# GpSimd's additions of squares behind the input and the mixing stages, and a wait in front of them

## The chip, the cores and the metric

The kernel runs on one core of one Trainium2 chip. The metric is the device time of one execution in microseconds, as the median of several runs. Names of the engines: TensorE (PE in the profile, PEld for its weight loads), VectorE (DVE), ScalarE (ACT), GpSimd (POOL), SyncE (SP, which issues the loads of weights here).

## The reference

Two small transformer blocks of two layers each, one after the other, on 256 tokens of width 1024 in float32. Cut to what matters here, a layer is

```python
def _rms(x, gain):
    y = x * rsqrt(mean(x * x, axis=-1) + EPS)
    return y * gain

x = x + 0.5 * swiglu(_rms(x, g0), w_in, w_out)      # feed-forward, hidden width 2816
x = x + mixing(_rms(x, g1))                         # a mixing stage
x = x + 0.5 * swiglu(_rms(x, g2), w_in, w_out)      # feed-forward
```

The four mixing stages are a gated linear recurrence (HGRN), a dilated attention, a stick-breaking attention and a sliding-window attention with sinks. Every norm needs the sum of the squares of the 1024 columns of x, for each token.

## The kernel before, in words

**Layout.** x lies transposed in SBUF, 8 chunks of 128 columns by 256 tokens, and is worked on in four pairs of chunks (NPAIR = 4). Float32 products are made of float32r parts: every operand is split into a high part and a low part (value less high part), and a product is high times high, high times low and low times high.

**Weights.** SyncE loads a stage's weights slot by slot, each slot in two halves, into `raw`. ScalarE copies a half into its high part (`split_high`, line 1304, tile `whi`), VectorE subtracts it to get the low part (`split_low`, line 1724, tile `wlo`, an operation on `raw` and `whi`). TensorE waits for the low part of the half that it is to use. The split of a slot is made two slots ahead of its use.

**Norm.** The scale of a norm is applied behind the product. So the input of a stage is only x times the gain: ScalarE makes its high part (`high_x`, line 1311, tile `xg`), VectorE its low part (`low_x`, line 1742, tile `xg`; operands x, the gain and the high part), chunk by chunk, and each low part raises the semaphore `xg_ready`. TensorE waits in the first slot of a stage for chunk after chunk. Beside it ScalarE squares each pair of chunks (line 1316): pair 0 into `acc`, pairs 1 to 3 into `sq`, `sq_two` and `newton`. GpSimd adds the three onto `acc` (`add_squares`, line 2227). TensorE sums `acc` over the partitions with a product with ones (`sum_squares`, lines 851 and 852), which waits for all additions. VectorE and ScalarE then make the reciprocal root `r` (lines 1748, 1324, 1326, 1752 to 1756).

**Behind a mixing stage** (and behind the input) comes a feed-forward. The four pairs of the output product come out shortly after one another at the end of the last output slot. VectorE adds pair m to x (line 1731; behind the input it is the copy of line 1729), then makes the two low parts of pair m-1, and behind pair 3 those of pairs 2 and 3. After them come, in VectorE's order, both weight halves of the second up slot (line 1724), the first half of the third, the sum of the first slot's gate (line 1797), which frees the first slot's bank, the second half of the third slot, the norm, the scaled gate (line 1802), a step of the sigmoid (line 1806), the first half of the fourth slot, and the sum of the second slot (line 1809), which frees the second slot's bank. The fourth slot uses that bank again. TensorE has `sum_squares` in the middle of the second up slot, between its two halves. An up slot is 8 chunks by 2 pairs of products (lines 839 and 840), 16 pairs in all.

**Behind a feed-forward** the pairs come out one by one, some 15 us apart, and GpSimd adds each as it comes (line 2227, called from `ffn`).

**GpSimd's order.** It adds the squares of the input first, and then goes through the layers; the adds of a mixing stage are the last of its work there, and the next on it is the gate work of the feed-forward behind (lines 2235, 2238, 2240), which waits for `r`. It issues no DMA.

Of the kernel before, what the change touches and what calls it, by code (L numbers as in the profile page):

```python
# [28 lines left out]
KC = D // P  # L29
# [4 lines left out]
NPAIR = KC // 2  # L34
# [98 lines left out]
def build_program(nc, io, upto=None):  # L133
# [6 lines left out]
    def sem(name):  # L140
        return ctx.enter_context(nc.semaphore(name))
# [56 lines left out]
    updates = [(n, us) for n, us in updates if n == "input" or n in stages]  # L198
    updates[-1] = (updates[-1][0], [])
    update_of = {name: e for e, (name, _) in enumerate(updates)}  # L200
    LAST = len(updates) - 1
    g_before, k_before = [], []
    for e in range(LAST + 1):
        g_before.append(KC * sum(u[0] == "g" for _, us in updates[:e] for u in us))
        k_before.append(KC * sum(u[0] == "k" for _, us in updates[:e] for u in us))
# [126 lines left out]
    xg_ready = sem("xg_ready")  # L332
# [51 lines left out]
    def pair(ap):  # L384
        return ap.rearrange("p (c t) -> p c t", c=2)

    def r_of(e):

        return r[:, e % 2:e % 2 + 1, :].broadcast_to([P, 2, T])

    def hidden(i, part):

        return hT[:, bass.ds(2 * i, 2), part, :]
# [1825 lines left out]
    def _(pool):  # L2219
# [3 lines left out]
        def add_squares(e, m):  # L2223

            pool.wait_ge(acc_done, NPAIR * e + m)
            pool.wait_ge(sq_done, (NPAIR - 1) * e + m)
            nc.gpsimd.tensor_tensor(acc[:, :], acc[:, :], squares_of[m][:, :], ALU.add).then_inc(acc_done, 1)  # L2227

        def ffn(f):
            st, e = stages[f"up{f}"], reads[f"up{f}"]  # L2230
            pool.wait_ge(r_ready, e + 1)
            with pool.Fori(0, FPAIRS) as i:
                p = FPAIRS * f + i
                pool.wait_ge(gate_made, p + 1)
                nc.gpsimd.tensor_tensor(pair(gate_r[:, :]), pair(gate[:, :]), r_of(e), ALU.mult).then_inc(gr_done, 1)  # L2235
                pool.wait_ge(gr_done, p + 2)
                pool.wait_ge(sig_ready, p + 1)
                nc.gpsimd.tensor_tensor(gate_s[:, :], gate_r[:, :], gate_s[:, :], ALU.mult).then_inc(gs_done, 1)  # L2238
                pool.wait_ge(hhi_done, p + 1)
                nc.gpsimd.tensor_tensor(hidden(i, 1), pair(h[:, :]), hidden(i, 0).bitcast(F32), ALU.subtract).then_inc(hT_ready, 1)  # L2240
            for m in range(1, NPAIR - 1 if update_of[f"down{f}"] == LAST else NPAIR):
                add_squares(update_of[f"down{f}"], m)

        def out_stage(name):
            for m in range(1, NPAIR):
                add_squares(update_of[name], m)

        def hgrn():
            nc.gpsimd.memset(hg_P[:, :, :], 0.0).then_inc(hg_zero, 1)
# [3 lines left out]
            for t in range(HG_TICKS):  # L2253
# [25 lines left out]
                for u in hg_units(t, 0):  # L2279
                    pool.wait_ge(hg_on, 2 * u + 2)  # L2280
                    pool.wait_ge(hg_gs, u + 1)
                    out = flat(hg_out[:, 2 * u:2 * u + 2, :])
                    nc.gpsimd.tensor_tensor(out, out, hg_g[:, :], ALU.mult).then_inc(hg_og, 1)
            out_stage("hgrn_out")


        def dil():
            st = stages["dil"]
            for point in range(2 * DL_TICKS):
                for hd in dl_due(point, DL_SCALE):  # L2290
                    pool.wait_ge(dl_rd, hd + 1)
                    own = dl_S[:, hd % 2, GROUPS * T:]
                    nc.gpsimd.tensor_tensor(own, own, dl_rcp[:, hd % 2, 0:1].broadcast_to([P, GROUPS * P]), ALU.mult).then_inc(dl_sc0, 1)
            out_stage("dil_out")


        def stick():
            out_stage("stick_out")
# [20 lines left out]
                    nc.gpsimd.tensor_tensor(own, own, sw_rcp[:, (u - 1) % 2, 0, :].unsqueeze(2).broadcast_to([P, 4, P]), ALU.mult).then_inc(sw_sc0, 1)  # L2319
            out_stage("swa_out")  # L2320

        for m in range(1, NPAIR):
            add_squares(0, m)
        for layer in layers:
            if layer.startswith("ffn"):
                ffn(int(layer[3:]))
            if layer == "hgrn":
                hgrn()
            if layer == "dil":
                dil()  # L2330
            if layer == "stick":
                stick()
            if layer == "swa_kv":
                swa_kv()
            if layer == "swa":
                swa()
# [34 lines left out]
```

## Time and profile before

| | us |
|---|---|
| median of 3 runs | 2165.11 |
| lowest, highest | 2163.71, 2165.37 |
| span of the profiled execution | 2161.0 |
| TensorE busy | 2126.5 (98%) |
| VectorE busy | 1607.5 (74%) |
| ScalarE busy | 1307.3 (60%) |
| GpSimd busy | 586.1 (27%) |

The profiled execution has no other time of its own than its span, from the first instruction to the last; the median of the runs is 4.1 us above it. How to read it: TensorE is almost never idle, so what matters is its few idle stretches. The row of the chain that ended last gives 90% of the span to TensorE, 5% to VectorE, 3% to ScalarE and 1% to GpSimd. A row of a timeline has the start, the duration (both in us), the engine, the line, the operation, the tiles written and read, the count of merged instructions, and in brackets the idle time before it with its releaser.

### The profile page before, as it was taken

To read this page: it belongs to the slowest core of one execution; us is meant where nothing else is said; L and a number is where in the kernel's file an instruction comes from. 1 tells how busy PE (TensorE), PEld (TensorE's weight loads), DVE (VectorE), ACT (ScalarE), POOL (GpSimd) and SP (SyncE) were. 2 spreads that over 40 slices of the span, in tenths; PEclk is the share of its full clock that TensorE was granted. 3 is DMA by queue.
4 is the path that set the end of the run, shared out by engine and by line. 5 is a ranking of instruction groups with operands and counts; after the bars stand their busy time and mean duration, and the time that the engine had idled before them with its cause. 6 is when DMAs were issued, how large, how long until landed. Compare 5 with 4: busy or idle time off the path is not lost.

```text
span 2161.0 us, 39632 instructions
## 1 busy us (share of the span) xinstructions
PE 2126.5 (98%) x14203; PEld 1920.3 (89%) x14203; DVE 1607.5 (74%) x1915; ACT 1307.3 (60%) x1815; POOL 586.1 (27%) x450
## 2 busy tenths in 40 slices
PE   8999899999999999999999999999999999999998
PEld 7889899888888899999888888999888888888887
DVE  7875888886887676766887687665887688677874
ACT  6664776664665565665665566475665466456663
POOL 3431672440342000000442243000342144122430
PEclk9999999999999999999999999999999999999999
DMA  6665467666566555554566567544566566534673
GB/s 211 193 199 180 128 191 259 193 209 189 166 194 212 165 172 162 160 160 150 168 194 211 158 194 220 159 145 149 177 192 212 158 191 202 187 108 150 191 221 100
DMA packets 371157, 387.92 MB, mean 180 GB/s; under 512 B 11334, under 2 KB 366031, under 8 KB 371056
## 3 DMA queue, kind: packets, MB, share of 16 engines
q1 hardware_dynamic: 357104, 369.14, 54.9%
q10 hardware_dynamic: 13952, 17.41, 2.5%
q8 instruction: 66, 1.08, 0.2%
q14 instruction: 35, 0.29, 0.0%
HBM read 376.02 MB, written 10.49 MB: 179 GB/s over the span
## 4 chain that ended last, share of the span: by engine, by line
PE 90%; DVE 5%; ACT 3%; POOL 1%; issue 1%; DMA 0%; ACTq 0%; DVEq 0%
PE ps L839 44%; PE ps L840 23%; PE ps L793 3%; PE ps L794 3%; PE ps L795 3%; PE ps L814 2%; PE ps L815 1%; PE ps L816 1%; DVE xg L1742 1%; PE ps L883 1%; DVE wlo L1724 1%; PE ps L885 1%; PE ps L884 1%; PE ps L1056 1%; PE ps L1024 1%
## 5 line engine op out<-in xcount | busy, mean ns | idle before, releaser
L1724 DVE TENSOR_TENSOR wlo<-raw,whi 128x1024 fp32r<-128x1024 f32 (+2 forms) x652 | 883.1, 1364 | 153.7 <-ACT whi L1304 152.6
L839 PE MATMUL ps<-xg,whi 128*128 128x512 f32 x2816 | 981.8, 392 | 4.1 <-DVE xg L1742 1.9
L1304 ACT ACTIVATE whi<-raw 128x1024 fp32r<-128x1024 f32 (+2 forms) x652 | 720.6, 1113 | 190.5 <-PE ps L840 130.2
L840 PE MATMUL ps<-xg,wlo 128*128 128x256 f32 x2816 | 794.5, 282 | 0.0
L839 PEld LDWEIGHTS ps<-xg,whi 128*128 128x128 f32 x2816 | 529.2, 188 | 118.3 <-DVE xg L1742 3.9
L840 PEld LDWEIGHTS ps<-xg,wlo 128*128 128x128 f32 x2816 | 532.9, 189 | 0.2
L839 PE MATMUL ps<-hT,whi 128*128 128x512 f32 x1408 | 488.5, 390 | 0.0
L840 PE MATMUL ps<-hT,wlo 128*128 128x256 f32 x1408 | 397.1, 282 | 0.0
L839 PEld LDWEIGHTS ps<-hT,whi 128*128 128x128 f32 x1408 | 264.3, 188 | 55.4
L2235 POOL TENSOR_TENSOR gate_r<-gate,r 128x512 f32<-128x512 f32 x88 | 189.6, 2155 | 286.5 <-DVE gate L1802 286.5
L840 PEld LDWEIGHTS ps<-hT,wlo 128*128 128x128 f32 x1408 | 266.1, 189 | 0.0
L793 PE MATMUL ps<-xg,whi 128*128 128x256 f32 x576 | 164.7, 286 | 3.2 <-DVE wlo L1724 3.2
L794 PE MATMUL ps<-xg,whi 128*128 128x256 f32 x576 | 160.8, 279 | 0.0
L2240 POOL TENSOR_TENSOR hT<-h,hT 128x512 f32 x88 | 117.3, 1333 | 159.8 <-ACT hT L1357 159.8
L795 PE MATMUL ps<-xg,wlo 128*128 128x256 f32 x576 | 160.6, 279 | 0.0
L2238 POOL TENSOR_TENSOR gate_s<-gate_r,gate_s 128x512 f32<-128x512 f32 x88 | 114.9, 1306 | 155.9 <-ACT gate_s L1351 155.9
L1820 DVE SCALAR_TENSOR_TENSOR x<-ps,x 128x512 f32<-128x512 f32 x32 | 22.1, 692 | 157.1 <-PE ps L840 157.1
L1346 ACT ACTIVATE gate_e<-gate 128x512 f32<-128x512 f32 x88 | 55.7, 633 | 137.2 <-DVE gate L1802 137.2
L1806 DVE TENSOR_SCALAR gate_e<-gate_e 128x512 f32<-128x512 f32 x88 | 129.6, 1472 | 5.6 <-ACT gate_e L1346 5.6
L2227 POOL TENSOR_TENSOR acc<-acc,sq 128x512 f32<-128x512 f32 x13 | 18.2, 1401 | 369.9 <-ACT sq L1316 369.9
L793 PEld LDWEIGHTS ps<-xg,whi 128*128 128x128 f32 x576 | 108.3, 188 | 7.0 <-issue 4.9
L1311 ACT ACTIVATE xg<-x,gains 128x256 fp32r<-128x256 f32 x96 | 43.4, 500 | 110.2 <-DVE x L1822 102.1
(286 smaller groups left out, 3067.2 us busy)
## 6 DMA issues: line engine op xcount, KB each, us to landing
raw<-in_ffn_w_in SPq DMA_DIRECT2D x352, 512.0 KB, 3.5
raw<-in_ffn_w_out SPq DMA_DIRECT2D x64, 768.0 KB, 4.7
raw<-in_ffn_w_out SPq DMA_DIRECT2D x64, 640.0 KB, 4.7
raw<-in_w_kv SPq DMA_DIRECT2D x48, 512.0 KB, 3.6
raw<-in_a_w_in SPq DMA_DIRECT2D x32, 512.0 KB, 4.5
raw<-in_b_w_q SPq DMA_DIRECT2D x24, 512.0 KB, 3.8
raw<-in_sb_w_qkv SPq DMA_DIRECT2D x24, 512.0 KB, 3.9
bias_by_distance<-bias_rows ACTq DMA_DIRECT2D x12, 768.0 KB, 5.0
```

The lines of the kernel that those rows point to most:

```text
L793: nc.tensor.matmul(out, whi[:, par, w], hi[:, k, :], start=k == 0 and m == 0, stop=False)
L794: nc.tensor.matmul(out, whi[:, par, w], lo[:, k, :], start=False, stop=False)
L795: mm = nc.tensor.matmul(out, wlo[:, par, w], hi[:, k, :], start=False, stop=k == total - 1 and m == 1)
L839: nc.tensor.matmul(out, whi[:, par, w], both, start=first and k == 0, stop=False)
L840: mm = nc.tensor.matmul(out[:, 0:T], wlo[:, par, w], both[:, 0:T], start=False, stop=last and k == total - 1)
L1304: nc.scalar.activation(whi[:, par, off:off + size], raw[:, 2 * par + half, :size], ACT.Copy).then_inc(hi_done, 1)
L1346: nc.scalar.activation(gate_e[:, :], gate[:, :], ACT.Exp, scale=-1.0).then_inc(gate_exp, 1)
L1724: nc.vector.tensor_tensor(wlo[:, par, off:off + size], raw[:, 2 * par + half, :size], whi[:, par, off:off + size].bitcast(F32), ALU.subtra ...
L1806: nc.vector.tensor_scalar(gate_e[:, :], gate_e[:, :], EXP_MAX, 1.0, ALU.min, ALU.add).then_inc(gate_den, 1)
L2235: nc.gpsimd.tensor_tensor(pair(gate_r[:, :]), pair(gate[:, :]), r_of(e), ALU.mult).then_inc(gr_done, 1)
L2238: nc.gpsimd.tensor_tensor(gate_s[:, :], gate_r[:, :], gate_s[:, :], ALU.mult).then_inc(gs_done, 1)
L2240: nc.gpsimd.tensor_tensor(hidden(i, 1), pair(h[:, :]), hidden(i, 0).bitcast(F32), ALU.subtract).then_inc(hT_ready, 1)
```

## The change

In front of the three additions behind the input and behind each of the four mixing stages GpSimd waits until all eight low parts of the normed input are there. The additions themselves, their order and all other waits stay. The additions behind the feed-forwards are not touched.

```diff
+        def add_all_squares(e):
+
+            pool.wait_ge(xg_ready, g_before[e] + KC)
+            for m in range(1, NPAIR):
+                add_squares(e, m)
+
@@
         def out_stage(name):
-            for m in range(1, NPAIR):
-                add_squares(update_of[name], m)
+            add_all_squares(update_of[name])
@@
-        for m in range(1, NPAIR):
-            add_squares(0, m)
+        add_all_squares(0)
```

`g_before[e]` is the number of low parts made ahead of update e, and KC = 8.

## Rows read from the trace of the kernel before

**Rows 1.** The page: busy time of each engine; TensorE's granted clock in 40 slices.

```profile
PE 2126.5 (98%) x14203; PEld 1920.3 (89%) x14203; DVE 1607.5 (74%) x1915; ACT 1307.3 (60%) x1815; POOL 586.1 (27%) x450
...
PEclk9999999999999999999999999999999999999999
```

**Rows 2.** Line 1742: instructions of one form, ns min/median/max, first and last start.

```profile
L1742 DVE SCALAR_TENSOR_TENSOR xg<-x,gains,xg x96: 468/480/1612, 10.8 to 1970.6; 128x256 fp32r<-128x256 f32 x96
```

**Rows 3.** Timeline of VectorE behind the dilated attention.

```profile
1027.68 4.40 DVE L1742 SCALAR_TENSOR_TENSOR xg<-x,gains,xg 128x256 fp32r<-128x256 f32 x4
```

**Rows 4.** Timeline of VectorE behind HGRN, low parts one by one.

```profile
357.34 1.14 DVE L1742 SCALAR_TENSOR_TENSOR xg<-x,gains,xg 128x256 fp32r<-128x256 f32 x1
...
358.40 1.52 DVE L1742 SCALAR_TENSOR_TENSOR xg<-x,gains,xg 128x256 fp32r<-128x256 f32 x1
```

**Rows 5.** Timeline of GpSimd behind HGRN.

```profile
356.90 1.30 POOL L2227 TENSOR_TENSOR acc<-acc,sq 128x512 f32<-128x512 f32 x1 [11.44 <-ACT sq L1316]
358.28 1.37 POOL L2227 TENSOR_TENSOR acc<-acc,sq_two 128x512 f32<-128x512 f32 x1
359.72 1.35 POOL L2227 TENSOR_TENSOR acc<-acc,newton 128x512 f32<-128x512 f32 x1
```

**Rows 6.** Timeline of TensorE behind HGRN; the last row is behind the input.

```profile
356.45 0.39 PE L839 MATMUL ps<-xg,whi 128*128 128x512 f32 x1
...
359.57 0.39 PE L839 MATMUL ps<-xg,whi 128*128 128x512 f32 x1
...
361.41 0.50 PE L839 MATMUL ps<-xg,whi 128*128 128x512 f32 x1 [0.47 <-DVE xg L1742]
...
362.99 0.47 PE L839 MATMUL ps<-xg,whi 128*128 128x512 f32 x1
...
375.02 0.39 PE L839 MATMUL ps<-xg,whi 128*128 128x512 f32 x1
...
32.45 0.39 PE L839 MATMUL ps<-xg,whi 128*128 128x512 f32 x1
```

**Rows 7.** Timeline of VectorE behind HGRN, 352 to 374 us.

```profile
355.95 0.87 DVE L1742 SCALAR_TENSOR_TENSOR xg<-x,gains,xg 128x256 fp32r<-128x256 f32 x2
...
361.67 3.48 DVE L1724 TENSOR_TENSOR wlo<-raw,whi 128x1024 fp32r<-128x1024 f32 x3
365.08 0.68 DVE L1797 TENSOR_TENSOR gate<-ps,gate 128x512 f32<-128x512 f32 x1
...
366.90 0.42 DVE L1748 TENSOR_SCALAR ms<-ps 128x256 f32<-128x256 f32 x1
...
373.85 0.69 DVE L1809 TENSOR_TENSOR h<-ps,h 128x512 f32<-128x512 f32 x1 [0.64 <-ACT h L1354]
```

**Rows 8.** Timeline of ScalarE behind HGRN.

```profile
357.98 0.89 ACT L1311 ACTIVATE xg<-x,gains 128x256 fp32r<-128x256 f32 x2
...
359.30 1.04 ACT L1304 ACTIVATE whi<-raw 128x1024 fp32r<-128x1024 f32 x1
```

**Rows 9.** Timelines of GpSimd and VectorE in the feed-forward behind HGRN.

```profile
376.45 1.34 POOL L2240 TENSOR_TENSOR hT<-h,hT 128x512 f32 x1 [1.68 <-ACT hT L1357]
...
377.15 1.73 DVE L1724 TENSOR_TENSOR wlo<-raw,whi 128x1024 fp32r<-128x1024 f32 x1 [0.51 <-ACT whi L1304]
```

**Rows 10.** Timeline of VectorE and GpSimd behind the input.

```profile
16.13 1.21 DVE L1724 TENSOR_TENSOR wlo<-raw,whi 128x1024 fp32r<-128x1024 f32 x1
16.15 2.34 POOL L2227 TENSOR_TENSOR acc<-acc,newton 128x512 f32<-128x512 f32 x1 [0.63 <-ACT newton L1316]
...
17.26 1.91 DVE L1742 SCALAR_TENSOR_TENSOR xg<-x,gains,xg 128x256 fp32r<-128x256 f32 x2
```

**Rows 11.** Timelines of TensorE, ScalarE and VectorE behind the input.

```profile
17.39 0.50 PE L839 MATMUL ps<-xg,whi 128*128 128x512 f32 x1 [0.59 <-DVE wlo L1724]
...
20.49 1.06 ACT L1304 ACTIVATE whi<-raw 128x1024 fp32r<-128x1024 f32 x1 [2.58 <-issue]
...
31.38 0.69 DVE L1809 TENSOR_TENSOR h<-ps,h 128x512 f32<-128x512 f32 x1 [0.63 <-ACT h L1354]
```

## The prediction

> **What bounds the kernel now.** I read the page first: TensorE is busy 2126.5 of 2161.0 us and its granted clock is at nine tenths or more in every slice, so 34.5 us of idle time are all that an edit on GpSimd can take from or add to [rows 1]. Since the change touches five places only, I then read the timelines of VectorE, ScalarE, GpSimd and TensorE around them, to see which wait ends last in each. The four places behind the mixing stages are copies of one another: the four low parts of the normed input that meet GpSimd's additions take 4.40 to 4.41 us at each of them, where each alone takes 0.48 us [rows 2, 3]. I work out the one behind the HGRN stage and multiply by four, then the one behind the input.
>
> The reader is to see three things there. First, the price of meeting an addition: the low part that starts at 357.34 takes 1.14 us and the next 1.52, because each runs into the addition of 1.30 to 1.37 us that GpSimd has going [rows 4, 5]. Second, TensorE pays for it: its pairs of products come every 0.347 us ((359.57 - 356.45) / 9), so its second slot of the up projection (16 pairs a slot) would start at 356.45 + 16 x 0.347 = 362.0, but starts at 362.99 [rows 6]. The loss of 0.97 us is the wait for a low part up to 361.41 and then for the low half of the weights, which VectorE starts at 361.67 and ends 1.21 later, at 362.88 [rows 6, 7]. The step from VectorE's end to TensorE's start is thus 0.1 us. Third, what comes after has little room: TensorE's fourth slot starts at 375.02 and needs the bank that VectorE empties at line 1809, from 373.85 to 374.54 [rows 6, 7]. Less 0.1 for the step, that is 0.38 us of room. Everything between (third weight half, gate sum, fourth weight half, the mean square at 366.90, Newton steps, gate) is one chain on VectorE and ScalarE that starts with the three weight halves at 361.67 [rows 7].
>
> **Removed.** The low parts no longer meet an addition. The last needs its high part, made by ScalarE at 357.98 + 0.89 = 358.87 [rows 8]; with some 0.05 for the step (my estimate, between none and the 0.1 above) and 0.48 for itself it ends at 359.4, not just ahead of 361.75. TensorE reaches that chunk at 356.45 + 14 x 0.347 = 361.3, so these waits go: it could start its second slot at 362.0, a gain of up to 0.97. ScalarE's squares are made at the same times as now, as they wait for the sum on VectorE that lies ahead of the low parts; its first high half of weights starts at 359.30 and is there at 360.34 [rows 8].
>
> **Added.** GpSimd waits for the last low part and then adds three times. Behind the waiting additions on GpSimd is only the next feed-forward's gate work, at 370 us and later, and nothing is queued for DMA there; the cost is whom the additions meet. They start at 359.4 + 0.1 = 359.5 to 359.65, and the first ends at 360.8 to 360.95. VectorE wants to make the low half of the weights at 360.38. That is an operation with both inputs in SBUF, and the trace shows what the pair costs, in both orders. A weight half that started at 377.15 under an addition of GpSimd's ending at 377.79 took 1.73 instead of 1.21: it began in effect 0.1 to 0.2 before that end [rows 9]. An operation of GpSimd that started at 16.15 under a weight half (16.13, 1.21 long) took 2.34 instead of 1.30: it began in effect at 17.19, 1.06 after VectorE's start [rows 10]. Whoever waits gets the next turn: in that case VectorE's next operation, at 17.26, waited, taking 1.91 for a pair that takes 0.87 elsewhere [rows 7, 10].
>
> So the two engines take turns: weight half, addition, weight half, addition, weight half. One turn of both costs 1.06 + 1.30 - 0.16 = 2.20 us where VectorE's pitch alone is 1.14 (363.95 - 361.67 is two of them; the third half ends 3.48 after 361.67) [rows 7]. The halves start in effect at 360.75, 362.95 and 365.15, the additions end at 363.1 and 365.3 after the first. The third half starts now at 361.67 + 3.48 - 1.21 = 363.94, so it comes 1.2 us later (1.1 to 1.35 by the ends of the starting time and of the turn). All that follows on VectorE is a chain and moves with it: gate sum, fourth half, mean square, and the emptying of the bank, to 374.54 + 1.2 = 375.74.
>
> The Trainium skill, SBUF — State Buffer, section Who interferes with whom, states that a VectorE instruction with two SBUF inputs contends with a GpSimd instruction that reads SBUF, and that the one issued first holds the shared ports "for the whole instruction" while the other fully blocks. It speaks against this change, as it names the weight halves as victims just like the low parts. Taken literally a turn would be 1.21 + 1.30 = 2.51 us and the cost of the four stages some 2.5 us higher than by the rows; the rows show the waiting one begin 0.1 to 0.2 before the holder's recorded end, and I go by them.
>
> **TensorE's side.** Its second slot needs the first weight half, 361.96 + 0.1: on time for 362.0 within 0.05. After half the slot, at 364.8, it wants the sum of squares, and the last addition ends at 365.3: a stall of 0.5 where there was none. Its fourth slot could now start some 0.4 earlier than before, but the bank is free at 375.74 + 0.1 = 375.84, against 375.02 before: 0.8 us later. A restart costs a little more: the first product after a wait takes 0.50 instead of 0.39 [rows 6], which is 0.1. Behind that I see no further wait: TensorE is by then 0.9 late itself, so a VectorE that is 1.2 late stands only 0.3 nearer to it than now, less than the room of 0.38. The early gain of 0.97 is thus wasted in front of a later wait, and **each mixing stage costs 0.9 us** (0.7 to 1.1). Four: +3.6.
>
> **The input.** Here additions meet low parts one by one; the last takes 2.34, and TensorE waits for a weight half until 17.39 [rows 10, 11]. Without these meetings VectorE ends the low parts at about 16.4 instead of 19.17, and TensorE's second slot could start 1.0 earlier. The additions then take turns with the halves from 16.4 on. The third half is held back here by ScalarE, whose high half comes at 20.49 + 1.06, or up to 0.9 earlier [rows 11], so VectorE has an idle gap that takes in one addition. If VectorE gets the first turn, the last addition ends near 23.3 and meets only the fourth half; the chain is then where it is now, and TensorE waits for the sum of squares at 23.4 and loses 0.1. If GpSimd gets the first turn, the chain is 0.75 late and the fourth slot, 32.45 now, with its bank emptied by 31.38 + 0.69 = 32.07 [rows 6, 11], starts 0.5 to 0.6 late. I take +0.2; bounds -0.9 (all of the gain kept) to +0.6.
>
> **The sum** is +3.8 us on the profiled execution: 2161.0 to 2164.8. The median of the runs shown is 2165.11, 4.1 above the span; nothing at either end of the program changes, so I add the same 3.8: **2168.9 us**, or +0.18%.
>
> **Rivals.** (a) GpSimd does not give turns up: all three additions are ahead of the first weight half. They would end at 359.55 + 3 x 1.30 + 2 x 0.08 = 363.6, the first half at 364.7, and TensorE's second slot would start at 364.8, 1.8 late; with the input about +8, so 2173. For it: the three additions follow each other within 0.08 us today [rows 5]. Against it: between them a low part gets its turn each time, since 1.14 and 1.52 are one wait each and not two [rows 4]. It decides slower from the moment that the first half waits for more than one addition. (b) The weight halves hide the additions: VectorE, which is busy back to back, keeps its pace, and the additions slip into its gaps. Then the third half is even earlier than now, TensorE keeps 0.97 at each stage and 0.9 at the input: -4.8, so 2160.3. Against it stand the 1.73 at 377.15 and the 1.91 at 17.26 [rows 9, 10]. (c) Turns as forecast, but the chain has more room than I see, or an addition falls into a gap as at the input: the early gain and the late wait cancel, within 1.5 us of 2165.1. The price of 0.9 is the difference of a shift of 1.2 and a room of 0.4, so half a turn less (one of the three additions unmet) makes it nearly nothing. (d) That the added wait does nothing can be left out: the first addition starts at 356.90, while low parts are still to be made from 357.34 on [rows 4, 5].
>
> **Chances.** Forecast 0.62, (a) 0.10, (b) 0.10, (c) 0.18. About 0.2%, or 4.3 us, is what a measurement of this kernel can tell from no change, and my forecast lies just inside it: of its 0.62, 0.25 go beyond the line. Slower 0.25 + 0.10 = 0.35; faster 0.06, since (b) passes the line only if nearly all of it is had; the same 0.59. Range: (c) and the forecast with its bounds (4 x 0.7 - 0.9 to 4 x 1.1 + 0.6, and 0.9 of scatter between runs), 2164.8 to 2171.0; it leaves out (a) and (b).
>
> **What would show it.** Right: low parts of 0.48 us behind the mixing stages; TensorE's second slot 5.6 us after the first; weight halves of about 2.2 us beside additions of about 2.2; a TensorE wait of about 0.5 ahead of the sum of squares, and one of 1.1 to 1.3 for VectorE's line 1809 ahead of the fourth slot, at four places. Wrong: weight halves of 1.21 there (then b), a first half that waits past 361.5 (then a), or no wait for line 1809 (then c).

## The result, and the profile after

The changed kernel takes 2166.41 us (median of 21 runs, 2166.07 to 2167.31), the kernel before 2163.71 us beside it (21 runs, 2162.49 to 2165.38): +2.7 us. The ratio is 1.0013 with a 95% interval of 1.0007 to 1.0018, which is 1.5 to 3.9 us. It is a small slowdown, inside the 0.2% that the forecast called no change, and on the side that it named. The profiled execution has a span of 2164.6 us, 3.6 more than the one of before; it took 2166.39 us as a whole, so 1.8 us lie around a span.

First VectorE behind HGRN. The columns are start, duration (us), engine, line, operation, tiles, and the idle time ahead with its releaser. The first product of the stage starts at 356.81 in this trace and at 356.45 in that of before [rows 6], so 0.36 is to be taken off when its times are set beside those of before.

```profile
357.65 0.87 DVE L1742 SCALAR_TENSOR_TENSOR xg<-x,gains,xg 128x256 fp32r<-128x256 f32 x2
358.82 0.89 DVE L1742 SCALAR_TENSOR_TENSOR xg<-x,gains,xg 128x256 fp32r<-128x256 f32 x2 [0.30 <-ACT xg L1311]
360.69 5.95 DVE L1724 TENSOR_TENSOR wlo<-raw,whi 128x1024 fp32r<-128x1024 f32 x3 [0.99 <-ACT whi L1304]
366.57 0.68 DVE L1797 TENSOR_TENSOR gate<-ps,gate 128x512 f32<-128x512 f32 x1
367.17 1.21 DVE L1724 TENSOR_TENSOR wlo<-raw,whi 128x1024 fp32r<-128x1024 f32 x1
368.30 0.41 DVE L1748 TENSOR_SCALAR ms<-ps 128x256 f32<-128x256 f32 x1
...
375.21 0.69 DVE L1809 TENSOR_TENSOR h<-ps,h 128x512 f32<-128x512 f32 x1 [0.63 <-ACT h L1354]
```

The four low parts take 0.87 and 0.89 a pair, where the four took 4.41 in before, with 1.14 and 1.52 for single ones [rows 4], and the three weight halves 5.95 instead of 3.48 [rows 7]. The cost has moved from one to the other. GpSimd's side:

```profile
359.78 1.30 POOL L2227 TENSOR_TENSOR acc<-acc,sq 128x512 f32<-128x512 f32 x1 [14.09 <-ACT newton L1316]
361.16 2.16 POOL L2227 TENSOR_TENSOR acc<-acc,sq_two 128x512 f32<-128x512 f32 x1
363.40 2.15 POOL L2227 TENSOR_TENSOR acc<-acc,newton 128x512 f32<-128x512 f32 x1
```

The second and third addition take 0.85 longer than the 1.30 of one that meets nothing: a half goes ahead of each, and each makes the next half wait. TensorE's side (the number of merged instructions closes a row):

```profile
356.81 0.40 PE L839 MATMUL ps<-xg,whi 128*128 128x512 f32 x1
...
362.36 0.39 PE L839 MATMUL ps<-xg,whi 128*128 128x512 f32 x1
...
365.61 0.70 PE L851 MATMUL ps<-acc,cst 128*128 128x256 f32 x2 [0.32 <-POOL acc L2227]
...
376.04 0.49 PE L839 MATMUL ps<-xg,whi 128*128 128x512 f32 x1 [0.97 <-DVE h L1809]
```

The second up slot starts 5.55 us after the first (6.54 before), so the early gain of 0.99 is there. Then TensorE waits for the sum, and then for line 1809 ahead of the fourth slot. The summary of TensorE's waits over the whole span (us in total, times, longest) has the wait for line 1809 at four places, and that for the sum at five, as the input is one of them. In before there is no entry for line 1809; there are four for low parts (line 1742), 1.9 us together:

```profile
PE ps L839 <- DVE h L1809: 3.9, 4, 1.0
PE ps L851 <- POOL acc L2227: 3.1, 5, 1.8
```

### The profile page after: what moved, and what is told of

Read it like the earlier page. It is cut to its first block, busy times and chain, and to the rows that moved or that the text cites. A ratio compares the mean times of both kernels' runs of the same rounds, so it can differ in the third digit from the quotient of the medians.

```text
span 2164.6 us, 39632 instructions
## 1 busy us (share of the span) xinstructions
PE 2128.0 (98%) x14203; PEld 1922.3 (89%) x14203; DVE 1606.0 (74%) x1915; ACT 1306.9 (60%) x1815; POOL 593.8 (27%) x450
## 4 chain that ended last, share of the span: by engine, by line
PE 87%; DVE 5%; ACT 4%; issue 1%; POOL 1%; DMA 0%; DVEq 0%; ACTq 0%; SPq 0%; POOLq 0%
PE ps L839 42%; PE ps L840 22%; PE ps L793 3%; PE ps L794 3%; PE ps L795 3%; DVE wlo L1724 2%; PE ps L814 2%; PE ps L815 1%; PE ps L816 1%; PE ps L883 1%; PE ps L885 1%; PE ps L884 1%; PE ps L1056 1%; ACT whi L1304 1%; PE ps L1024 1%
## 5 line engine op out<-in xcount | busy, mean ns | idle before, releaser
L1724 DVE TENSOR_TENSOR wlo<-raw,whi 128x1024 fp32r<-128x1024 f32 (+2 forms) x652 | 894.9, 1382 | 157.5 <-ACT whi L1304 156.3
L839 PEld LDWEIGHTS ps<-xg,whi 128*128 128x128 f32 x2816 | 528.7, 188 | 118.3 <-issue 7.2
L793 PEld LDWEIGHTS ps<-xg,whi 128*128 128x128 f32 x576 | 109.6, 190 | 6.8 <-issue 4.9
L794 PEld LDWEIGHTS ps<-xg,whi 128*128 128x128 f32 x576 | 109.6, 190 | 0.8 <-issue 0.5
```

What stands on the lines that cost most here:

```text
L793: nc.tensor.matmul(out, whi[:, par, w], hi[:, k, :], start=k == 0 and m == 0, stop=False)
L794: nc.tensor.matmul(out, whi[:, par, w], lo[:, k, :], start=False, stop=False)
L839: nc.tensor.matmul(out, whi[:, par, w], both, start=first and k == 0, stop=False)
L1724: nc.vector.tensor_tensor(wlo[:, par, off:off + size], raw[:, 2 * par + half, :size], whi[:, par, off:off + size].bitcast(F32), ALU.subtra ...
```

## The experiments

Times are medians beside the kernel before in the same set. The table shows for each kernel where TensorE is behind the dilated attention: the start of its 17th (second slot), 25th (behind the sum), 49th (fourth slot) and 65th pair of products, in us after the 1st. The other mixing stages agree with it within 0.08, but for e9 behind HGRN. "Gap" means that one step of VectorE is moved into the time in which it waits for ScalarE's root. The intervals of e6, e7, e8 and e11 hold 1, so their times alone don't tell them from before; what is said of them rests on the columns of the traces.

| kernel | 17th | 25th | 49th | 65th | against before, us | ratio, 95% interval |
|---|---|---|---|---|---|---|
| before | 6.51 | 10.03 | 18.55 | 24.09 | | |
| after | 5.55 | 9.60 | 19.27 | 24.91 | +2.7 | 1.0007 to 1.0018 |
| e4, no additions | 5.55 | 9.00 | 17.51 | 23.06 | -4.9 | 0.9966 to 0.9986 |
| e5, fills | 5.55 | 9.00 | 17.51 | 23.06 | -5.3 | 0.9965 to 0.9985 |
| e6, after + gap | 5.55 | 9.61 | 18.25 | 23.90 | -0.6 | 0.9986 to 1.0004 |
| e7, before + gap | 6.51 | 10.04 | 18.55 | 24.10 | -0.1 | 0.9989 to 1.0007 |
| e8, third late | 5.68 | 9.63 | 18.14 | 23.69 | -1.6 | 0.9984 to 1.0002 |
| e9, e8 + gap | 5.69 | 9.64 | 18.15 | 23.70 | -2.3 | 0.9980 to 0.9998 |
| e10, third after low parts + gap | 5.68 | 9.13 | 17.64 | 23.19 | -3.6 | 0.9974 to 0.9992 |
| e11, e10 without gap | 5.69 | 9.14 | 18.17 | 23.82 | -1.1 | 0.9985 to 1.0003 |

**The change again.** The file is unchanged.

> The changed kernel again, beside the others of this set. Theory T: behind each mixing stage the additions and VectorE's weight halves take turns, the chain up to line 1809 comes 1.0 to 1.2 us late, and TensorE waits for the bank ahead of the fourth up slot; 0.7 us lost at each of four places, nothing at the input: +2.8 us against before (2 to 3.6). Theory S: what costs is that the sum of squares is late, so that TensorE waits ahead of line 851. For this run both give the same number.

2166.57 us against 2163.68: +2.9, ratio 1.0004 to 1.0022. The fifth slot (65th pair) lies 24.92 after the first, 0.8 later than in before. Four times 0.8 are 3.2 us, slightly more than the difference of the medians.

**No additions.**

```diff
             pool.wait_ge(xg_ready, g_before[e] + KC)
-            for m in range(1, NPAIR):
-                add_squares(e, m)
+            pool.wait_ge(sq_done, (NPAIR - 1) * (e + 1))
+            pool.wait_ge(acc_done, NPAIR * e + 1)
+            pool.sem_inc(acc_done, NPAIR - 1)
```

> Leaves out the three additions behind the input and behind each mixing stage (the sum is then that of the first pair's squares alone); all signals are given at the same places. Prices both kernels' meetings at once. Theory T: no low part and no weight half meets anything there, the third weight half comes 1.2 us earlier than in before, TensorE's second up slot starts 0.97 us earlier at the four mixing stages and 0.9 to 1.0 at the input, and nothing takes it back: -4.8 us against before (-4 to -5.5). If the low parts cost TensorE nothing in the end (something later takes the gain back at once), 0 to -1.

2158.79, -4.9: theory T's number. The meetings cost the kernel before 1.03 us at each mixing stage (24.09 - 23.06) and the changed one 1.85. No wait for line 1809, 851 or 1742 is left in TensorE's summary. As GpSimd still waits for the low parts here, the wait itself isn't what costs.

**Fills in place of additions.**

```diff
             for m in range(1, NPAIR):
-                add_squares(e, m)
+                pool.wait_ge(acc_done, NPAIR * e + m)
+                pool.wait_ge(sq_done, (NPAIR - 1) * e + m)
+                nc.gpsimd.memset(squares_of[m][:, :], 4000.0)
+                nc.gpsimd.memset(acc[:, :], 4000.0).then_inc(acc_done, 1)
```

> Like the changed kernel, but in place of each addition GpSimd fills the two operands with a constant (two fills of 128x512, which read nothing), so it is busy at the same place for about as long (some 1.1 us for each), and the sum of squares comes out of the constant. Tells whether it is the reading of the additions that VectorE's weight halves meet, or any work of GpSimd. Theory T with reading: weight halves of 1.21 us, no wait for line 1809, about as without additions: -4.8 us against before (-4 to -5.5). If any GpSimd operation makes VectorE wait: near the changed kernel, +1.5 to +3.

2158.37, -5.3, with the same table row as no additions at all; one wait of 0.7 us for line 1809 is left, behind the input. VectorE and GpSimd behind HGRN:

```profile
359.48 3.50 DVE L1724 TENSOR_TENSOR wlo<-raw,whi 128x1024 fp32r<-128x1024 f32 x3 [0.98 <-ACT whi L1304]
...
358.56 0.52 POOL L2235 MEMSET sq<- 128x512 f32 x1 [14.00 <-ACT newton L1316]
359.02 0.53 POOL L2236 MEMSET acc<- 128x512 f32 x1
...
361.13 0.52 POOL L2236 MEMSET acc<- 128x512 f32 x1
```

GpSimd is busy from 358.56 to 361.65, and the three halves take 3.50, as if it were idle. So it isn't GpSimd's being at work that they meet, and not the added wait, but something that an addition has and a fill has not. That this is the reading is the likeliest, but the two differ in length too (1.30 and 0.52), and no run has another operation of GpSimd that reads. It agrees with what the Trainium skill states in SBUF — State Buffer, section Who interferes with whom: an operation of VectorE with two inputs in SBUF contends with one of GpSimd that reads SBUF, not with one that only writes it. One bound: the fills end at 361.65, while the third addition ends at 365.55, so a part of the difference could be the shorter time of contact; the first two halves, from 359.48 to 361.8, did overlap the fills and show no delay at all.

**VectorE's step moved into the norm's gap, on the changed kernel and on the one before.** This is the run that tells the chain from the late sum.

```diff
                 if first:
-                    split_low(*ahead_of(st, i, 0), (1,))
-                    stage_norm(f"up{f}")
+                    stage_norm(f"up{f}", lambda: split_low(*ahead_of(st, i, 0), (1,)))
```

> The changed kernel with one step of VectorE's order moved in the first pass of each feed-forward: the second weight half of the third up slot is made behind the mean square (line 1748), in the 0.9 us in which VectorE waits for ScalarE's root, instead of ahead of it. The additions meet the same halves, and the sum of squares is as late as in the changed kernel. Theory T (the chain over line 1748 to line 1809 sets the loss): the chain comes 0.9 us earlier, the wait for line 1809 goes, and the loss with it: -0.3 us a mixing stage against before, so -1 us (-2 to 0), and -3.7 against the changed kernel. Theory S (the late sum costs): nothing moves, +2.7 against before.

> The kernel before with VectorE's one step moved as in e6_after_gap (the second weight half of the third up slot behind the mean square). The control for it. Theory T: in before the chain has 0.4 us of room up to the bank and its mean square waits for the sum anyway, so the move is worth nothing there: 0.0 us against before (-0.5 to +0.5). If the move were worth something in itself (fewer waits in every feed-forward), e6's 3.5 us would not be proof of T, and this one would be 1 us or more faster.

On the changed kernel 2163.05, -0.6 against before (so 3.5 less than the changed kernel); on the kernel before 2163.79, -0.1. VectorE with the moved step, behind HGRN (first product at 357.67), and TensorE's fourth slot:

```profile
361.60 5.94 DVE L1724 TENSOR_TENSOR wlo<-raw,whi 128x1024 fp32r<-128x1024 f32 x3 [0.98 <-ACT whi L1304]
367.46 0.68 DVE L1797 TENSOR_TENSOR gate<-ps,gate 128x512 f32<-128x512 f32 x1
368.06 0.41 DVE L1748 TENSOR_SCALAR ms<-ps 128x256 f32<-128x256 f32 x1
368.39 1.21 DVE L1724 TENSOR_TENSOR wlo<-raw,whi 128x1024 fp32r<-128x1024 f32 x1
369.52 0.41 DVE L1752 SCALAR_TENSOR_TENSOR newton<-r 128x256 f32<-128x256 f32 x1
...
375.92 0.49 PE L839 MATMUL ps<-xg,whi 128*128 128x512 f32 x1
```

The three halves are as slow as in the changed kernel (5.94), and TensorE waits for the sum as long (25th pair at 9.61). Only the chain from the gate sum to the mean square is 1.1 shorter, and the fourth slot comes at 18.25 instead of 19.27. A wait of 0.1 for line 1809 is left. So the late sum alone costs nothing against before, though it takes 0.6 of the early gain (9.00 without additions); the loss comes by the chain up to line 1809. In the kernel before the same move is worth nothing, as its chain had room.

**The wait behind the input alone.** The changed kernel with `out_stage` as in before.

```diff
         def out_stage(name):
-            add_all_squares(update_of[name])
+            for m in range(1, NPAIR):
+                add_squares(update_of[name], m)
```

> The wait behind the input alone; the mixing stages are as in before. Tells what share of the change's cost is the input's. Theory T: the early gain is given back ahead of the sum of squares, 0.0 us against before (-0.5 to +0.3). If the four stages carry less than their reckoned 2.8 us, the rest would show here, +0.5 or more.

2163.74 against 2163.86: nothing, ratio 0.9989 to 1.0008. The cost is that of the four mixing stages.

**Two additions as before, the third behind the first weight half, without and with the gap.**

```diff
-            pool.wait_ge(xg_ready, g_before[e] + KC)
             for m in range(1, NPAIR):
+                if m == NPAIR - 1:
+                    pool.wait_ge(lo_done, 2 * (stages[stage]["base"] + 1) + 1 + 4)
                 add_squares(e, m)
```

(`stage` is the up stage behind update e.)

> At the five places the first two additions run as in before, beside the low parts, and only the third waits, for the low half of the first weight half behind them (second up slot, first half). Theory T: two low parts still meet an addition but the third does not, the first weight half ends by 362.0 in the HGRN case and meets nothing, the third addition meets one half; the bank is free 0.1 us later than in before, so TensorE, which could be 0.9 earlier, gets only the 0.4 of room less a restart: -0.2 us a mixing stage, -0.8 against before (-1.8 to 0).

> e8_third_late together with VectorE's step moved as in e6_after_gap. Theory T: now neither end of the chain takes the gain back: low parts and first weight half are in time, and the bank is free 0.9 us earlier. 0.85 us at each mixing stage (a wait of 0.1 for the sixth low part stays), nothing at the input: -3.4 us against before (-2.5 to -4.5), faster than both kernels. If the limit were elsewhere, it would stay at e8's time.

-1.6 and -2.3. The first lies in its range, but not by the mechanism that was expected: TensorE doesn't wait for line 1809 there at all (its 49th pair comes 8.51 after the 25th, as without additions). The second fell short of its -3.4: at three of four mixing stages the moved step changed nothing (23.69 and 23.70), so the limit was elsewhere. The trace of e8 behind the dilated attention shows it:

```profile
1031.34 3.48 DVE L1724 TENSOR_TENSOR wlo<-raw,whi 128x1024 fp32r<-128x1024 f32 x3
...
1032.63 3.35 POOL L2227 TENSOR_TENSOR acc<-acc,newton 128x512 f32<-128x512 f32 x1 [2.29 <-DVE wlo L1724]
```

The third addition was asked for at 1032.63, 0.15 after the second half had begun, and took 3.35: it let two halves pass, not one, and VectorE's three halves lost nothing (3.48). It ended at 1035.98, and the 25th pair came at 9.63, 0.5 later than in e10 below, where the sum is in time. Behind HGRN in e9 it won the turn instead, with the halves at 4.59 and the addition at 2.21, and there the 25th pair came at 9.12. Seven of the eight mixing stages of e8 and e9 go as the one shown, and this is the eighth. So the strict taking of turns, on which my reckoning rests, isn't a rule.

**The third addition behind the last low part, with and without the gap.**

```diff
-                    pool.wait_ge(lo_done, 2 * (stages[stage]["base"] + 1) + 1 + 4)
+                    pool.wait_ge(xg_ready, g_before[e] + KC)
```

> What e9_third_late_gap left: there the third addition, asked for 0.14 us after the second weight half had begun, waited for two halves in four of five stages, and TensorE waited for the sum (its 25th pair 9.6 us after the first instead of 9.1). Here the third addition waits for the last low part instead, so it is asked for one half earlier; the step of VectorE is moved as there. Theory T: even if it waits for two halves it ends by the time that TensorE wants the sum; the 25th pair comes 9.1 us after the first (10.05 in before), the 49th after 17.6 (18.55), so 0.9 us at each mixing stage: -3.7 us against before (-2.8 to -4.5). If the wait for the sum was not what e9 lacked, it stays at e9's -2.3.

> The same without VectorE's moved step: one addition of three waits for the low parts, where the changed kernel makes all three wait. Theory T: the first weight half starts about 1 us earlier than in before, since one low part fewer meets an addition, and one half is delayed by 1.1, so the chain up to line 1809 is where it is in before; TensorE gets the room and no more: -0.3 us a mixing stage, -1.2 against before (-2.2 to -0.3). The loss of the changed kernel would so lie in the second and third meeting. If the order alone (any addition behind the low parts) cost, it would be slower than before.

-3.6 and -1.1, both as expected; e10 takes 2159.92 us and is faster than both kernels (0.9974 to 0.9992 of before). Behind the dilated attention in e10:

```profile
1029.13 3.37 DVE L1742 SCALAR_TENSOR_TENSOR xg<-x,gains,xg 128x256 fp32r<-128x256 f32 x4
1032.42 4.59 DVE L1724 TENSOR_TENSOR wlo<-raw,whi 128x1024 fp32r<-128x1024 f32 x3
...
1032.58 2.21 POOL L2226 TENSOR_TENSOR acc<-acc,newton 128x512 f32<-128x512 f32 x1 [1.16 <-DVE xg L1742]
```

One meeting is spent on the low parts less than in before (3.37 instead of 4.40), one on the halves (4.59 instead of 3.48), and the sum is in time. Without the gap the chain is where it was in before: TensorE waits for line 1809 at four places in e11, 1.4 us in all. So a wait in front of one addition does no harm. The changed kernel's loss comes with moving the other two as well; no run moves two of three.

## Why the prediction was right, point by point

- **What bounds, and the removed meetings: right.** The low parts end without a meeting, and the second slot starts 5.55 after the first, where 5.55 was reckoned.
- **The taking of turns: right for this kernel.** 2.16 and 2.15 for the additions where 2.2 was said, and 2.24 from the start of one to that of the next (363.40 - 361.16), nearer to the 2.20 by the rows than to the 2.51 of the rival reading. (The words "for the whole instruction", which the prediction quotes from the Trainium skill, SBUF — State Buffer, section Who interferes with whom, stand there on VectorE's two-port modes; for the shared ports in general the section has an exclusive lock.) The third half came 1.13 later than in before (366.57 - 356.81 against 365.08 - 356.45, both for what follows it), where 1.2 was said. e8 shows that it is no rule. Why an addition asked for 0.15 us behind the start of a half lost its turn at seven of eight mixing stages in e8 and e9 and won it at one stays open.
- **The step that was mis-sized: the shift of the chain.** I let 1.2 pass on to line 1809. It was 1.00 (375.21 - 356.81 against 373.85 - 356.45). 0.07 of the difference is the third half's. Another 0.09 went at the mean square, whose start moved by 1.04: in before it had the sum to wait for as well as the fourth half, and in the changed kernel it starts 0.08 ahead of that half's recorded end (368.30 against 367.17 + 1.21). The last 0.04 went on ScalarE's part of the chain.
- **TensorE: right.** The sum brought the 25th pair 0.6 later than it comes without additions (9.60 against 9.00; 0.5 said), of which 0.32 is recorded as a wait. The wait ahead of the fourth slot was 1.15 (1.50 between pairs instead of 0.35), where 1.1 to 1.3 was said, and the restart added 0.1 behind it. So the loss is 0.7 at the 49th pair and 0.8 at the 65th, against 0.9 said.
- **The input: right.** +0.1 in the trace (the 49th pair 20.20 after the first, against 20.06), with the longest wait for the sum, 1.8, taking an early gain of the same size. The second slot started 1.9 earlier in this trace and 1.0 in e1's, where 1.0 was reckoned; the 25th pair came at 11.7 in both. e2 is within noise of nothing; +0.2 was said. VectorE did get the first turn (16.31, the addition 16.37).
- **The base: wrong by 1.4.** I added the difference to a median of three runs, 2165.11, and took the 4.1 us between it and the span for something around the program. Only 1.8 lie there. The rest was the spread between executions: the profiled one stood at about 2161.0 + 1.8 = 2162.8, and the median of 21 runs is 2163.71, 1.4 below that of the first three. The difference of 2.7 against the 3.8 forecast is the other part of what separates 2168.9 from 2166.41.
- **The range.** Its low end of 2164.8 doesn't come out of its own terms: the forecast's bounds give 2165.1 + 1.9 - 0.9 = 2166.1, and (c) alone 2163.6. The measured time lies 0.3 above the first of these, so it is within the range either way. The 4.3 us that a measurement was thought to need was too much: 21 runs of each told 2.7 from nothing.
- **The rivals.** (a) fell: the first half ran 0.3 after it could. (b) fell for the changed kernel by the 5.95 of the halves, but its price was right: with the meetings gone the kernel takes 4.9 less. (c) by its time alone isn't out, since 2166.41 is within 1.5 us of 2165.1, partly because of the base; what rules it out is the wait for line 1809 at four places, which it said would be missing. e11, with one meeting moved instead of three, comes out as (c) said of one addition fewer.
- **What is left.** The two traces differ by 3.6 us. Four stages at 0.8 and the input's 0.1 make 3.3, and the medians' +2.7 agrees with that within its interval. The rest of the traces' difference, 0.3, lies inside the HGRN mixing stage (356.81 against 356.45 at its end), where nothing was changed. There TensorE's granted clock differs between the two traces (stretch, sum, busy time and count of PE, PEld, DVE, ACT and POOL, granted clock, DMA share, GB/s; two rows of before, then two of after):

```profile
226.00:230.00 4.00, 4.00 (x37) 4.00 (x36) 3.97 (x5) 1.94 (x4) 4.00 (x6) 1.00 0.65 188
254.00:257.00 3.00, 3.00 (x26) 2.93 (x25) 2.97 (x3) 2.19 (x4) 3.00 (x5) 0.94 0.81 263
...
226.00:230.00 4.00, 4.00 (x23) 4.00 (x23) 3.96 (x5) 1.95 (x4) 4.00 (x6) 0.57 0.68 203
254.00:257.00 3.00, 3.00 (x16) 2.88 (x15) 3.00 (x3) 2.25 (x5) 3.00 (x5) 0.51 0.86 275
```

TensorE fell over 1 us behind in the first of these stretches, and later waits took most of that up again; that the 0.3 is what they left is likely, but not shown. The spread of the kernel before goes with the clock as well: of its 29 runs beside e1, the four with a mean granted clock of 0.998 took 2162.40 to 2163.38 us, and the nine with 0.996 took 2163.55 to 2165.42.

## What to carry to other kernels

An operation that two engines must not run together is not made free by moving it behind the critical operation: ask which operation of the same kind comes next, and follow the chain behind it to the first place where the bounding engine waits. Here three meetings moved from the low parts, where they cost TensorE 1.03 us a mixing stage together, to the weight halves, where they cost 1.85. What gained here was to split the work (e10): two additions on one side and one on the other, as each had room, and a step that waits for nothing moved into the gap of the chain.

## What the runs showed of the hardware that I had not expected

- An addition of GpSimd that asks while VectorE works through three weight halves back to back can let two of them pass (3.35 us for 1.30), or one (2.21), from nearly the same starting point, 0.15 us after a half's start. It let two pass at seven of eight mixing stages.
- Two fills of GpSimd (0.52 us each) beside VectorE's halves cost these nothing: 3.50 us for three.
- In the profiled execution of e10 TensorE stood idle for 1.97 us behind the input, up to 17.43, and its granted clock then fell from 1.00 to 0.50 (1.2 GHz instead of 2.4), where it stood from 18 to 20 us; its pairs came every 0.64 us until 21.1. This execution took 2161.57 us, 1.65 above the kernel's median; two more of its eleven lie beside it, at 2161.33 and 2161.51. That these two had the same drop is not shown. Nor is a drop peculiar to this kernel or place: behind the input e2 and e4 stood at 0.50 from 14 to 16 us and e8 from 15 to 17, after 1.98, 1.95 and 1.82 us of idle time ahead of the first pair, and the kernel before has 0.62 from 250 to 254 us, which the page's 40 slices of 54 us don't show. One thing stays open: in before the first pairs behind the input (12.39 to 15.09) came every 0.64 to 0.78 us as well, with the clock recorded as 1.00; the wait for a weight half up to 17.39 [rows 11] hid what that cost. The columns are the stretch, the sum, busy time and count of each engine, the granted clock, the DMA share and GB/s:

```profile
16.00:18.00 2.00, 0.57 (x3) 0.52 (x4) 2.00 (x4) 1.93 (x3) 0.00 (x0) 0.97 0.62 215
18.00:20.00 2.00, 2.00 (x8) 1.71 (x7) 2.00 (x3) 0.00 (x0) 1.75 (x1) 0.50 0.66 194
...
22.00:24.00 2.00, 2.00 (x14) 1.76 (x13) 1.39 (x2) 1.55 (x2) 0.00 (x0) 1.00 0.98 305
```
